# Layer 1 of a two-layer encoder trunk: queries before memory queries, and both attentions spread behind three weight streams

## The reference, cut to what matters

```python
proj = u @ swa_w_in[j]                     # queries 1024, keys 256, values 256, memory queries 512
y_mix = swa_sink_attention(q, k, v, sinks, rel_bias)   # 16 heads of 64; a query block of 64 tokens
                                                       # sees its own 64 keys and the 64 before
y_mem = memory_cross_attention(q_mem, mem_kv)          # 4 heads of 128 over 256 memory tokens
mixed = jnp.concatenate([y_mix, y_mem], axis=-1) @ w_out
h = h + rmsnorm(mixed, norm_mix_post[i])
```

## Time and profile before

| what | us |
|---|---|
| median of three runs (lowest, highest) | 1431.06 (1429.76, 1431.58) |
| the profiled execution | 1434.14 |
| its span, first to last instruction | 1432.4 |
| PE busy in the span | 1369.3 (96%) |
| DVE, ACT busy | 697.2 (49%), 578.1 (40%) |
| mean granted TensorE clock | 0.985 of full |

### The profile page before, as it was taken

One profiled execution on the slowest core, in us unless ns is written; L12 is line 12 of the kernel. 1 busy time (PEld: TensorE's weight loads), 2 busy tenths in 40 slices (PEclk: granted clock), 3 DMA queues, 4 the chain that ended last, 5 costly groups with the idle time before them and its releaser, 6 DMA issues.

```text
span 1432.4 us, 18082 instructions
## 1 busy us (share of the span) xinstructions
PE 1369.3 (96%) x6775; PEld 1134.5 (79%) x6775; DVE 697.2 (49%) x1088; ACT 578.1 (40%) x1091; POOL 121.2 (8%) x133
## 2 busy tenths in 40 slices
PE   6989999989999999999999999977999999999998
PEld 5778878888768888888888888755888888888886
DVE  5566676777434634223443455566356442234333
ACT  5635455656433534223332343445335332134321
POOL 0033444551000000000000000000000000000000
PEclk9999999999999999999999999988999999999999
DMA  6252333332321232233232132100313322322322
GB/s 200 86 136 85 103 95 120 113 126 90 146 85 63 89 111 94 102 119 101 90 103 101 62 103 89 59 16 1 118 59 104 102 98 93 117 88 88 108 98 74
DMA packets 75485, 137.36 MB, mean 96 GB/s; under 512 B 6358, under 2 KB 16918, under 8 KB 75414
## 3 DMA queue, kind: packets, MB, share of 16 engines
q1 hardware_dynamic: 71184, 134.76, 28.8%
q10 hardware_dynamic: 4230, 1.63, 0.7%
HBM read 133.44 MB, written 2.93 MB: 95 GB/s over the span
## 4 chain that ended last, share of the span: by engine, by line
PE 82%; DVE 8%; ACT 4%; issue 2%; POOL 2%; DMA 2%; SPq 0%; ACTq 0%; DVEq 0%; POOLq 0%
PE G L1560 53%; PE X L1560 11%; PE X L1583 5%; PE X L1631 2%; POOL csrow L498 2%; DVE conv L1137 2%; DVE wlo L1010 2%; PE X L1995 1%; PE X L1810 1%; ACT whi L545 1%; PE G L1631 1%; PE X L1800 1%; DMA raw<-in_w_up 1%; DMA csrow<-cs_rows 1%; DVE ulo L1321 1%
## 5 line engine op out<-in xcount | busy, mean ns | idle before, releaser
L1010 DVE TENSOR_TENSOR wlo<-raw,whi 128x1024 fp32r<-128x1024 f32 x224 | 275.8, 1236 | 504.0 <-ACT whi L545 503.0
L545 ACT ACTIVATE whi<-raw 128x1024 fp32r<-128x1024 f32 x224 | 235.7, 1058 | 485.5 <-PE G L1560 276.5
L1560 PE MATMUL G<-uhi,whi 128*128 128x512 f32 x736 | 295.1, 401 | 1.9 <-DVE ulo L1027 1.8
L1560 PE MATMUL G<-uhi,wlo 128*128 128x512 f32 x736 | 287.3, 390 | 0.0
L1560 PE MATMUL G<-ulo,whi 128*128 128x512 f32 x736 | 287.1, 390 | 0.0
L1560 PEld LDWEIGHTS G<-uhi,whi 128*128 128x128 f32 x736 | 138.5, 188 | 33.1 <-issue 4.1
L1560 PEld LDWEIGHTS G<-uhi,wlo 128*128 128x128 f32 x736 | 138.3, 188 | 29.6
L1560 PEld LDWEIGHTS G<-ulo,whi 128*128 128x128 f32 x736 | 138.6, 188 | 28.1
L1560 PE MATMUL G<-whi,hidhi 128*128 128x512 f32 x256 | 99.6, 389 | 0.0
L1560 PE MATMUL G<-whi,hidlo 128*128 128x512 f32 x256 | 99.6, 389 | 0.0
L1560 PE MATMUL G<-wlo,hidhi 128*128 128x512 f32 x256 | 99.6, 389 | 0.0
(11 more groups left out here) (341 smaller groups left out, 2358.4 us busy)
## 6 DMA issues: line engine op xcount, KB each, us to landing
raw<-in_w_up SPq DMA_DIRECT2D x64, 512.0 KB, 3.8
raw<-in_w_down SPq DMA_DIRECT2D x64, 512.0 KB, 3.4
raw<-in_ssd_w_in SPq DMA_DIRECT2D x20, 512.0 KB, 3.6
raw<-in_w_mem_kv SPq DMA_DIRECT2D x16, 512.0 KB, 3.4
raw<-in_ssd_w_out SPq DMA_DIRECT2D x16, 512.0 KB, 3.4
raw<-in_swa_w_in SPq DMA_DIRECT2D x16, 512.0 KB, 3.8
raw<-in_ssd_w_in SPq DMA_DIRECT2D x16, 384.0 KB, 3.3
csrow<-cs_rows SPq DMA_DIRECT2D x16, 384.0 KB, 4.4
```

Source lines behind the costliest of these rows:

```text
L545: act.activation(whi[q][:, :, :], raw[q % 2][:, :, :], ACT.Copy).then_inc(hi_done, 1)
L1010: dve.tensor_tensor(wlo[q][:, :, :], raw[q % 2][:, :, :], whi[q][:, :, :].bitcast(F32), ALU.subtract).then_inc(lo_done, 1)
L1560: mm = pe.matmul(o, st, mv, start=(kt == 0 and fresh and not go_on), stop=(q == total - 1 and k == 1), skip_group_check=True)
```

## The change

Three edits. (1) Block B_QB (queries) comes before B_Q1 (memory queries), and the first four y tiles that the output projection takes are local attention's, not memory's. (2) Both attentions now run behind banks: a **slot** is one bank of six products, counted from B_QB's first (B_QB is slots 0 to 15, B_Q1 16 to 31, the first half of B_W1 32 to 55). Tables say which unit or memory step stands behind which slot: turns of units 0 to 7 behind slots 7, 8, 10, 11, 13, 14, 16, 17, of units 8 to 15 behind slots 23, 24, 26, 27, 29, 30, 32, 33, memory steps 0 to 7 behind 38, 39, 40, 42, 43, 44, 46, 47. Memory attention of layer 1 uses X in place of G. Copying the queries is shared: DVE banks 0 and 2, ACT banks 1 and 3; ACT copies the memory queries (qmT1). (3) In `memory_step` of both layers ACT does the exponentials of step n+1 before it copies step n, and DVE does the maxima of n+1 before it divides n.

```diff
-B_Q1, N_Q1 = 35, 29
-B_QB, N_QB = 36, 30
+B_QB, N_QB = 35, 29
+B_Q1, N_Q1 = 36, 30
...
-F_W0, F_F0, F_KV, F_QA, F_Q1, F_QB, F_W1, F_F1 = 13, 14, 24, 25, 26, 27, 28, 29
+F_W0, F_F0, F_KV, F_QA, F_QB, F_Q1, F_W1, F_F1 = 13, 14, 24, 25, 26, 27, 28, 29
+
+
+SLOT0 = 4 * B_QB
+W_TURN = {7 + 3 * u // 2: u for u in range(8)} | {23 + 3 * u // 2: 8 + u for u in range(8)}
+W_FIRST = {3: 0, 4: 1, 19: 8, 20: 9}
+W_LAST = {19: 7, 35: 15}
+M_FIRST = (35, 36)
+M_TURN = {38 + 4 * n // 3: n for n in range(2 * MH)}
+M_LAST = 49
...
-            for blk, c0 in ((B_QA, 0), (B_Q1, (QH + 2 * KVH) * CH), (B_QB, 512)):
+            for blk, c0 in ((B_QA, 0), (B_QB, 512), (B_Q1, (QH + 2 * KVH) * CH)):
...
-                load(v[(n + 4) % 6, n // 6], B_W1 + n // 4, n % 4)
+                load(v[n % 6, n // 6], B_W1 + n // 4, n % 4)
...
+                if n + 1 < 2 * MH:
+                    memory_exp(i, mp, B, n + 1)
                 act.wait_ge(ma_tr, 8 * i + n + 1)
                 act.activation(mpT[h % 2][:, :, 256 * tp:256 * tp + 256],
                                B[2][:, :].rearrange("p (m n) -> p m n", m=MT), ACT.Copy).then_inc(ma_pT, 1)
-                if n + 1 < 2 * MH:
-                    memory_exp(i, mp, B, n + 1)
...
+                    if m == 2:
+                        attention_panel(4 * blk + q)
+                        if q == 5:
+                            act.activation(eps[:, 4:5], eps[:, 0:1], ACT.Sqrt)
...
+            def attention_panel(p):
+
+                for slot in range(4 * (p - SLOT0), 4 * (p - SLOT0) + 4):
+                    u = W_LAST.get(slot)
+                    if u is not None:
+                        w_out(u)
+                    u = W_FIRST.get(slot)
+                    if u is not None and u % NCH == 0:
+                        w_exp(u)
+                    u = W_TURN.get(slot)
+                    if u is not None:
+                        if u % NCH < NCH - 1:
+                            w_exp(u + 1)
+                        w_turned(u)
+                        if u % NCH > 0:
+                            w_out(u - 1)
+                    if slot == M_FIRST[0]:
+                        memory_exp(1, mp1, X, 0)
+                    n = M_TURN.get(slot)
+                    if n is not None:
+                        memory_step(1, mp1, mpT1, ymhi1, X, n)
+                    if slot == M_LAST:
+                        memory_out(1, ymhi1, X, MH - 1)
...
+            def queries(n, blk, j):
+                for b in (1, 3):
...
             ahead(B_QA)
-            ahead(B_Q1, (0,))
-            w_exp(0)
-            for u in range(7):
-                ahead(B_Q1 + (u + 1) // 4, ((u + 1) % 4,))
-                w_step(u)
-            for u in range(7, 2 * NCH - 1):
-                w_step(u)
-                if u == 7:
-                    memory_exp(1, mp1, G, 0)
-                memory_step(1, mp1, mpT1, ymhi1, G, u - 7)
-            memory_out(1, ymhi1, G, MH - 1)
-            w_turned(2 * NCH - 1)
+            queries(N_QA, B_QA, 0)
+            for blk in (B_QB, B_Q1):
+                for q in range(4):
+                    ahead(blk, (q,))
+                    attention_panel(4 * blk + q)
+                if blk == B_QB:
+                    queries(N_QB, B_QB, 1)
+                else:
+                    for b in range(4):
+                        group_ready(act, N_Q1, 4 * B_Q1 + 4, b)
+                        act.activation(qmT1[:, b, :], G[b][:, :], ACT.Copy,
+                                       scale=float(P) ** -0.5).then_inc(bank_free[b], 1)
...
+                if n + 1 < 2 * MH:
+                    maxima(i, B, n + 1)
                 dve.wait_ge(ma_exp, 16 * i + 2 * n + 2)
                 link(dve.reciprocal(msum[:, 3, j:j + 2], msum[:, 2, j:j + 2]))
                 dve.tensor_tensor(mp[tp][:, :, :], mp[tp][:, :, :],
                                   msum[:, 3, j:j + 2].unsqueeze(2).to_broadcast([P, 2, M]), ALU.mult).then_inc(ma_p, 1)
-                if n + 1 < 2 * MH:
-                    maxima(i, B, n + 1)
...
-                for b in range(4):
+                for b in (0, 2):
...
+            def attention_panel(p):
+
+                for slot in range(4 * (p - SLOT0), 4 * (p - SLOT0) + 4):
+                    u = W_LAST.get(slot)
+                    if u is not None:
+                        w_lo(u - 1)
+                        w_lo(u)
+                    u = W_FIRST.get(slot)
+                    if u is not None and u % NCH == 0:
+                        w_scores(u)
+                    u = W_TURN.get(slot)
+                    if u is not None:
+                        if u % NCH < NCH - 1:
+                            w_scores(u + 1)
+                        w_norm(u)
+                        if u % NCH >= 2:
+                            w_lo(u - 2)
...
+            def attention_behind(blk):
 
                 def after_bank(q, b):
+                    slot = 4 * (4 * blk + q - SLOT0) + b
+                    u = W_LAST.get(slot)
+                    if u is not None:
+                        w_values(u)
+                    u = W_FIRST.get(slot)
+                    if u is not None:
+                        if u % NCH == 0:
                             for x in range(4):
+                                pe.wait_ge(bank_free[x], F_QA + u // NCH + 1)
+                        if u == 0:
                             pe.wait_ge(half_k, 2)
                             pe.wait_ge(half_v, 2)
+                        w_scores(u)
+                    u = W_TURN.get(slot)
+                    if u is not None:
+                        if u % NCH + 2 < NCH:
+                            w_scores(u + 2)
                         w_transposes(u)
                         if u == 1:
                             pe.wait_ge(v2_done, 2)
+                        if u % NCH > 0:
+                            w_values(u - 1)
+                    if slot == M_FIRST[0]:
+                        for x in range(4):
+                            pe.wait_ge(bank_free[x], F_Q1 + 1)
+                        pe.wait_ge(a_sb, 2 * NCH)
+                        memory_scores(1, qmT1, X, 0)
+                    elif slot == M_FIRST[1]:
+                        memory_scores(1, qmT1, X, 1)
+                    n = M_TURN.get(slot)
+                    if n is not None:
+                        if n == 0:
+                            pe.wait_ge(a_pT, 2 * NCH)
+                        if n == 2:
+                            pe.wait_ge(a_lo, 2 * NCH)
+                        memory_step(1, mp1, mpT1, qmT1, X, n)
+                    if slot == M_LAST:
+                        memory_values(1, mpT1, X, MH - 1)
                 return after_bank
...
+            gemm(N_QB, B_QB, 4, weights_still(u_of), u_wait(U0[3]), bank(F_QB), after_bank=attention_behind(B_QB))
+            gemm(N_Q1, B_Q1, 4, weights_still(u_of), u_wait(U0[3]), bank(F_Q1), after_bank=attention_behind(B_Q1))
...
+                if kt < 8:
+                    return y1hi[:, kt, rows], y1lo[:, kt, rows]
+                return ymhi1[:, kt - 8, rows], ymlo1[:, kt - 8, rows]
...
+                 after_bank=attention_behind(B_W1))
+            pe.wait_ge(ma_exp, 32)
+            pe.wait_ge(ma_pT, 4 * MH)
+            pe.wait_ge(ma_lo, 2 * MH)
```

More of the change, by code:

```diff
@@ new lines, in queries @@
+            def queries(n, blk, j):
+                for b in (1, 3):
+                    group_ready(act, n, 4 * blk + 4, b)
+                    for s in range(2):
+                        half = slice(CH * s, CH * s + CH)
+                        cp = act.activation(qT[:, 4 * j + b, :, s, :],
+                                            G[b][half, :].rearrange("p (c q) -> p c q", q=CH), ACT.Copy)
+                    cp.then_inc(bank_free[b], 1)
+            ahead(B_QA)
+            queries(N_QA, B_QA, 0)
@@ L1508, in w_lo @@
                                   y1hi[where].bitcast(F32), ALU.subtract).then_inc(a_lo, 1)
[L1510 to L1521, removed]
-                if u == 2:
-                    for b in range(4):
-                        group_ready(dve, N_Q1, 4 * B_Q1 + 4, b)
-                        dve.tensor_scalar(qmT1[:, b, :], G[b][:, :], float(P) ** -0.5, None,
-                                          ALU.mult).then_inc(bank_free[b], 1)
-            queries(N_QB, B_QB, 1)
-            for u in range(7, 2 * NCH - 1):
-                w_step(u)
-                if u == 7:
-                    maxima(1, G, 0)
-                memory_step(1, mp1, ymhi1, ymlo1, G, u - 7)
-                w_lo(u - 1)
-            w_norm(2 * NCH - 1)
-            memory_lo(1, ymhi1, ymlo1, G, MH - 1)
+            def attention_panel(p):
[15 more added lines that the diff above has]
+                    if slot == M_FIRST[0]:
+                        maxima(1, X, 0)
+                    n = M_TURN.get(slot)
+                    if n is not None:
+                        memory_step(1, mp1, ymhi1, ymlo1, X, n)
+                    if slot == M_LAST:
```

(36 more changed lines are left out.)

47 lines of the change are left out of this document (8 added, 39 removed).

## The result

| | before | after |
|---|---|---|
| median, us (lowest, highest) | 1431.32 (1429.76, 1433.05) | 1449.55 (1446.14, 1451.60) |
| the profiled execution | 1434.14 | 1450.39 |
| its span | 1432.4 | 1448.2 |
| mean granted clock | 0.985 | 0.981 |

The changed kernel is slower: ratio 1.0125, 95% interval 1.0101 to 1.0148, that is +18.2 us. The forecast was 1444 (+13).

A forecast was written before the change was run, and what follows sets the result against it. The 164.7 us stretch was taken as 16.4 waiting, 8.1 clock and 140.2 work; it becomes 140.9 work, 22.8 waits and 11.0 clock, 174.7 (+10.0). With layer 0's +3.3 on 1431.06 that gives 1444 us, range 1429 to 1452.

The forecast's parts named there:

- The waits of layer 1: In the changed stretch, casts in the path to the next transposes make PE wait 22.8 us, in place of 16.4.
- Work of the stretch: From B_QB's start to the output projection's first half, all products are kept; PE's work is 140.9 us, 140.2 before.
- the 7 extra excursions: Excursions between banks in the stretch rise from 24 to 31, at 0.1 us each: +0.7 us of work.
- The clock: In layer 1's stretch, half-rate work behind the new waits costs 11.0 us, bounds 5.4 and 16.8; before it was 8.1.
- the price list: Clock loss behind earlier waits: 4.0 us behind 5.1, 2.7 behind 4.4, 1.7 behind 1.8, nothing behind 2.0.
- The two large ones: Waits of 5.1 us at slots 16 and 32, expected to lose 6.7 us together to the clock.
- Layer 0: Memory steps: the next step's maximum adds 0.8 us to three waits, +2.4, and the clock 0.9: +3.3, bounds 0 and 6.
- Rival 1: Casts do not hold the transposes at panel starts; only slots 16 and 32 wait: 1426.5 us, chance 0.13.
- no waits at all: Case within Rival 1's chance of 0.13: the stretch has no waits, 1431 - 24 = 1407 us.
- Rival 2: Waits come as counted but the clock mostly stays up, losing 2.7 us: 1432.5 to 1435 us, chance 0.17.
- Rival 3: Every wait drops the clock at its upper price, 16.8 us, and layer 0 costs 6: 1453 us, chance 0.06.
- The two readings of the clock: Recurring gaps are each paid again in clock, or only longer gaps are, making the sum 4 us lower.

The follow-up runs named there:

- e3: Changed kernel with ScalarE's cast whi in front of pT, not behind it, at the turns behind slots 7, 11, 23 and 27: 1438.07 us.
- e5: Changed kernel with the casts of the panels beginning at slots 16 and 32 moved behind those panels' turns on ScalarE and VectorE: 1432.69 us.
- e6: e1 with all layer 1 casts moved to turns with two banks behind them, or behind the turns at slots 16 and 32: 1422.02 us.
- e9: e8 with y1lo put ahead of the cast wlo on VectorE, behind a unit's division: 1407.93 us.
- e1: Changed kernel with layer 0's memory step back in the old order, exponentials and maxima of the next step behind copy and division: 1444.56 us.
- e4: Changed kernel with idle products on TensorE ahead of the transposes of units 1, 6, 9 and 14: 1436.64 us.
- e8: e6 with VectorE's cast wlo behind the memory step and y copies in panels 1, 2, 5 and 6 of layer 0's output projection: 1416.75 us.

## Why the prediction was right, and where it was off

- **The waits of layer 1: right in place and size.** Forecast 22.8, measured 22.1. Per slot, forecast and measured: 8 and 24: 3.4, and 3.21 and 3.20; 13 and 29: 0.7, and 0.51 and 0.55; 16 and 32: 5.1, and 4.96 and 4.42; 40 and 44: 2.2, and 2.24 and 2.23. Slot 47 (0.82) was called covered and was not. The cause, the cast in an in-order list ahead of the work that PE needs, is shown by e3, e5, e6 and e9: moving casts (in e9, what stands behind one) took the waits away. The stated idle of VectorE before wlo is in the rows (3.55).
- **Work of the stretch.** Forecast 140.9; measured 156.65 - 18.0 = 138.7. Before it was 148.34 - 8.4 = 139.9, so the 7 extra excursions did not cost the 0.7 put down for them; why it is lower by 2 was not traced. These 2 us, and 0.7 in the waits, hid part of the miss that follows.
- **The clock: the term that was mis-sized.** "Sum 11.0, bounds 5.4 and 16.8": it was 18.0, above the upper bound. The step that failed is the price list drawn from the earlier trace rows. "Two of 3.4, between 1.7 and 2.7: I take the lower" was 3.0 and 3.4 each; "two of 2.2 ... I take 0.9 for both" was 1.7 each; and slots 13 and 29, for which nothing was put down, took 1.7 each. The two large ones came out lower: 3.15 and 1.7, against 6.7 together. I read a price per wait from the four waits of the earlier trace rows, and the trace of the kernel before had nearer ones. In its bare attention the clock fell behind 2.97 us (with 1.27 close behind it; 5.48 x 0.49 = 2.7 lost) and behind 0.82 (at 981.65; 1.7 lost):

```profile
994.31 0.66 PE L2020 MATMUL X<-ident,sc 128*128 128x128 f32 x4 [2.97 <-DVE sc L1500]
```

```profile
996.00:1003.00 7.00, 5.48 (x10) 2.89 (x11) 2.10 (x6) 2.89 (x11) 0.00 (x0) 0.51 0.00 0
```

Wait and clock together were 33.8 forecast, 40.1 measured. Why the clock fell behind every wait of this stretch but the last, and behind one of five in layer 0, no run shows. That waits stand close together is not enough: here one comes every 9 to 26 us, in layer 0 every 9 to 20.
- **Layer 0.** Forecast +3.3; e1's medians give 5.0, with some 3 us either side, and the traces 2.2 without a fall of the clock and 4.1 with the one in the changed kernel. The waits for mp grew by 2.85: 0.8 at each of three, as said, nothing at the last, and a new one of 0.47. The wait for y0lo shrank by 0.9, which was not foreseen. So the forecast was about right here.
- **The sum.** By the traces some 14 of the 18.2 are in layer 1 (the stretch is 14.1 longer) and 2 to 4 in layer 0, where 10.0 and 3.3 were forecast. Of the miss of 5, 4.1 is in the stretch: 7.0 of the clock, less the 2.9 by which work and waits were put too high. So the sum came out nearer than its clock term did, by luck.
- **The rivals.** Rival 1 (the casts do not hold the transposes) is refuted for the kernel as written: the transposes at slots 8 and 24 wait 3.2 us. That e9's 1408 is close to the 1407 named for "no waits at all" is chance: e9 still has 6.1 us of waits and a fall of 1.7 in the stretch, and its 1408 contains the gain in layer 0. Rival 2 (clock stays up) is refuted by the mean clock of 0.90 in the stretch. Rival 3 (every drop at its upper price) is nearest for the clock (16.8, measured 18.0), though its 6 for layer 0 was too much.
- **The two readings of the clock.** In layer 1 waits of 0.5 to 5 us that recurred were paid twice, and e4 takes most of the second payment away. The Trainium skill (TensorE: Matmul & The Clock Gate, HAM oscillation) has it, for waits of 3 to 5 us between short bursts, that the low clock is paid again behind each gap. The trace agrees in layer 1 (18.0 us behind 22.1 of waits) and not in layer 0 (1.7 behind 8.65). The reading by which the four waits of 2.2 and 3.4 us cost little, 4 us lower in the sum, was farther off, and was not quite what that page's table gives: it exempts the two of 2.2 only. The four lost 1.7, 1.7, 3.0 and 3.4.

## What to carry to other kernels

When small chains are spread behind a stream, follow each chain through every engine's list, and look for prefetch work (casts for a panel three ahead) that stands ahead of the chain's next step. Such work has much slack and the chain has none, so put it behind; e3, e5, e6, e8 and e9 each took off 5 to 23 us by position alone. A wait on TensorE may cost up to twice its length or more, by the clock that falls behind it; take the price from waits in the same kind of work, and put a range on it, since the same wait can be followed by a fall in one execution and not in the next. Check who else is queued behind the instruction that you move.

## What the runs showed of the hardware that was not expected

- The clock fell behind waits of 0.51 and 0.55 us in the changed kernel (914 to 919: 0.66), where earlier waits lay about 20 us back, and at the same two slots in e1, e4 and e5 (0.51 to 0.64). In e9 it stayed at 1.00 through waits of 0.56 and 0.57 and through four of 0.67 to 1.16 us, and fell once behind 1.55. The length of a wait alone does not decide it.
- Behind a wait of about 2 us that both kernels have, it falls in one execution and not in another. In the profile before it fell behind 2.26 (at 295), 1.81 (358), 1.91 (405) and 2.17 (473), and not behind 1.96 (830) and 2.00 (1080). After, it fell behind 2.61 (358), 2.07 (830) and 1.95 (1095), and not behind 2.27 (295), 1.90 (407) and 2.18 (473). Each fall takes some 1.6 us. They may be part of why the profiled execution before (1434.14) stood 3 us above its median; that was not shown. The eight falls in the changed kernel's stretch came again in e1, behind the same waits.
- Products that compute nothing, put where PE would have waited anyway, kept the clock up enough to save 12.9 us (e4).
